# Scan output products in one row shape, and modulation columns one round later, in a two-layer hybrid block

## What is computed

```
for layer in 0, 1:
    mods = silu(c) @ w_mod[layer] + b_mod[layer]        # 6 * 1024 values, for latent and for context
    h    = rmsnorm(x) * (1 + sc1) + sh1
    u, qa, ka, va, qn, kn, vn, gates = split(h @ w_in[layer])
    y    = readout(scan_forward(u)) + readout(scan_backward(u)) + d_skip * u    # 32 groups of 16 channels, 64 states
    branches = glu(y), attention(qa, ka, va), neighbourhood_attention(qn, kn, vn)
    x    = x + g1 * (gated_merge(branches, gates) @ w_out)
    x    = x + g2 * mixture_of_experts(rmsnorm(x) * (1 + sc2) + sh2)            # 16 experts, top 2
```

## Time and profile before

| | us |
|---|---|
| median of 3 runs | 1943.32 (1941.05 to 1944.64) |
| the profiled execution | 1942.77 |
| its span, first to last instruction | 1941.1 |
| PE busy | 1762.7 |
| mean granted TensorE clock | 0.952 of full |
| layer 0: z of round 1 starts | 196.35 |
| layer 0: z of round 5 starts, attention starts | 274.48, 329.92 |
| layer 1: z of round 1 starts, attention starts | 1286.13, 1401.45 |

### The profile page before, as it was taken

One profiled execution on the slowest core, in us unless ns is written; L12 is line 12 of the kernel. 1 busy time (PEld: TensorE's weight loads), 2 busy tenths in 40 slices (PEclk: granted clock), 3 DMA queues, 4 the chain that ended last, 5 costly groups with the idle time before them and its releaser, 6 DMA issues.

```text
span 1941.1 us, 25808 instructions
## 1 busy us (share of the span) xinstructions
PE 1762.7 (91%) x9800; PEld 1064.2 (55%) x9800; DVE 656.6 (34%) x1410; ACT 411.4 (21%) x846; POOL 337.1 (17%) x314
## 2 busy tenths in 40 slices
PE   5999998889999999999979798999789999997796
PEld 2567555554444444555546446766458886554463
DVE  4669442660110113211101367775281113110012
ACT  3111111552000003222212231111152002221122
POOL 0004352870000001100000110425291000000000
PEclk9999897999999999999999898999699999999898
DMA  9313258309221243699999421144543367999992
GB/s 387 109 44 114 76 189 296 85 23 349 106 108 65 94 188 130 250 389 345 387 395 388 140 86 66 44 168 139 196 63 126 135 250 280 346 383 394 386 380 89
DMA packets 113523, 397.32 MB, mean 205 GB/s; under 512 B 42992, under 2 KB 62448, under 8 KB 74256
## 3 DMA queue, kind: packets, MB, share of 16 engines
q1 hardware_dynamic: 55920, 327.04, 43.8%
q10 hardware_dynamic: 50720, 29.54, 6.2%
q0 software_dynamic: 6784, 39.33, 6.0%
HBM read 369.65 MB, written 38.80 MB: 210 GB/s over the span
## 4 chain that ended last, share of the span: by engine, by line
PE 61%; DMA 11%; DVE 10%; SPq 6%; POOL 5%; issue 4%; ACT 2%; ACTq 1%; POOLq 0%; DVEq 0%
PE tile_ps L547 54%; SPq L492 6%; DMA arena<-sorted_in 4%; PE turn_ps L547 4%; DMA ring<-in_wpack 3%; POOL arena L1724 2%; DMA vn<-in_wpack 2%; PE out_ps L547 1%; ACTq L1086 1%; DMA arena<-arena 1%; PE turn_ps L772 1%; DVE arena L1592 1%; DVE x L1659 1%; DMA x<-in_xT 1%; DVE rstd L1365 1%
## 5 line engine op out<-in xcount | busy, mean ns | idle before, releaser
L547 PE MATMUL tile_ps<-h,ring 128*128 128x512 f32 (+1 forms) x1312 | 471.9, 514 | 3.9 <-ACT h L965 1.9
L547 PEld LDWEIGHTS tile_ps<-h,ring 128*128 128x128 f32 x1312 | 249.1, 192 | 214.1 <-issue 198.8
L547 PE MATMUL tile_ps<-arena 64*16 64x128 f32 (+4 forms) x1984 | 257.4, 376 | 31.2 <-ACT arena L1180 11.4
L547 PE MATMUL tile_ps<-arena,ring 128*128 128x512 f32 (+1 forms) x704 | 235.4, 486 | 2.7 <-issue 2.7
L547 PEld LDWEIGHTS tile_ps<-arena 128*64 128x64 f32 (+3 forms) x1984 | 165.1, 162 | 95.1 <-issue 64.9
L547 PEld LDWEIGHTS tile_ps<-arena,ring 128*128 128x128 f32 x704 | 133.9, 190 | 96.3 <-issue 87.4
L1724 POOL TENSOR_SCALAR arena<-arena,smx 128x512 f32<-128x512 f32 (+1 forms) x96 | 129.0, 1360 | 81.4 <-DVE smx L1578 81.1
L547 PE MATMUL tile_ps<-ring,arena 128*64 128x256 f32 (+1 forms) x624 | 97.4, 454 | 11.3 <-ACT arena L1180 7.1
L1156 ACT ACTIVATE arena<-tile_ps 128x512 f32<-128x512 f32 (+1 forms) x56 | 27.4, 490 | 347.4 <-PE tile_ps L547 347.4
L1650 DVE TENSOR_TENSOR arena<-tile_ps,arena 64x256 f32<-64x256 f32 x40 | 16.6, 416 | 225.0 <-ACT arena L1177 225.0
L1613 DVE TENSOR_TENSOR arena<-tile_ps,arena 128x512 f32<-128x512 f32 (+1 forms) x32 | 17.9, 558 | 212.1 <-PE tile_ps L547 212.1
(11 more groups left out here) (272 smaller groups left out, 2259.1 us busy)
## 6 DMA issues: line engine op xcount, KB each, us to landing
ring<-in_wpack SPq DMA_DIRECT2D x176, 1024.0 KB, 8.5
arena<-in_wpack SPq DMA_DIRECT2D x64, 1024.0 KB, 17.4
h<-in_wpack SPq DMA_DIRECT2D x15, 1024.0 KB, 26.0
qa<-in_wpack SPq DMA_DIRECT2D x12, 1024.0 KB, 14.7
qn<-in_wpack SPq DMA_DIRECT2D x12, 1024.0 KB, 17.1
kn<-in_wpack SPq DMA_DIRECT2D x12, 1024.0 KB, 20.0
vn<-in_wpack SPq DMA_DIRECT2D x12, 1024.0 KB, 22.1
sorted_out<-arena ACTq DMA_DIRECT2D x80, 128.0 KB, 7.5
```

Of the source, the lines that this page charges most:

```text
L547: return nc.tensor.matmul(out, lhsT, rhs, start=start, stop=stop)
```

## The change

- The `tm` product of each group is cut in two over its rows: the lower 64 go into bank y, the upper 64 into bank yb. All products of y and yb are then over 64 rows, in pairs of a lower and an upper one. Their number rises from 40 to 48 instructions for a round.
- mc of this layer's block is moved from its own round to the next one, behind y and yb (in round 8, ahead of them). DVE's use of it moves too.
- mr of this layer's block is moved behind the projections of its round; ACT copies its rows behind the projections.
- The next layer's blocks in layer 0 (rounds 5 to 7) come ahead of this layer's mr, and block 3 comes in round 8 (mr ahead of the last y, mc behind it) and no longer in the attention.
- The list of banks and the order of the slots follow. A round of nine is z, z, y, yb, mc, qk_ms, projection, mr, rope.

```diff
-IN_ROUND = {5: 0, 6: 1, 7: 2}
-IN_STEP = {1: 3}
+IN_ROUND = {5: 0, 6: 1, 7: 2, 8: 3}
+
+def next_mod(l, q):
+    return [IN_ROUND[q]] if l + 1 < LAYERS and q in IN_ROUND else []
...
     (order of the slots)
-    for q in range(NQ):
-        steps += mod(l, MOD1 + q)
+    for q in range(NQ + 1):
+        for n in next_mod(l, q):
+            steps += mod(l + 1, n)
         for job in in_loop(fill, q):
             steps += projected(job)
+        if q < NQ:
+            steps += mod(l, MOD1 + q)
...
     (TensorE)
+                def late_modulation(q):
+                    modulation_columns(l, MOD1 + q - 1)
+                    for n in next_mod(l, q):
+                        modulation(l + 1, n, l)
...
+                    if q == NQ:
+                        late_modulation(q)
...
-                            mm(bank(fwd)[:, cols], tm[:, o % 2, g, :], ug[:, G, :], True, False)
+                            for d, to in ((lower, fwd), (upper, bwd)):
+                                mm(bank(to)[:, cols], tm[d, o % 2, g, :], ug[d, G, :], True, False)
...
-                                b = mm(bank(bwd)[:, cols], co[upper], s, r == 0, r == 1)
+                                b = mm(bank(bwd)[:, cols], co[upper], s, False, r == 1)
                         full(fwd, f)
                         full(bwd, b)
+                    if 0 < q < NQ:
+                        late_modulation(q)
...
-                    if q < NQ:
-                        modulation(l, MOD1 + q, l)
+                    for n in next_mod(l, q):
+                        modulation_columns(l + 1, n)
                     for job in in_loop(fill, q):
                         projection(job, c0)
                     if q < NQ:
-                        modulation_columns(l, MOD1 + q)
+                        modulation(l, MOD1 + q, l)
...
-                    if l + 1 < LAYERS and q in IN_ROUND:
-                        modulation(l + 1, IN_ROUND[q], l)
-                        modulation_columns(l + 1, IN_ROUND[q])
...
     (ScalarE)
+                    if q == NQ:
+                        for n in next_mod(l, q):
+                            copy_rows(l + 1, n)
                     if q:
                         job = (l, "y", q - 1)
                         copy(job, ...)
+                    if q < NQ:
+                        for n in next_mod(l, q):
+                            copy_rows(l + 1, n)
...
+                    for job in in_loop(fill, q):
+                        copy_projection(job, c0)
                     if q < NQ:
                         copy_rows(l, MOD1 + q)
-                    for job in in_loop(fill, q):
-                        copy_projection(job, c0)
```

More of the change, by code:

```diff
@@ L210, in tile_jobs @@
             names += [(l, "z", q, 0), (l, "z", q, 1)] if q < NQ else []
-            names += [(l, "y", q - 1), (l, "yb", q - 1)] if q else []
+            late = [(l, "mc", MOD1 + q - 1)] if q else []
+            late += [(l + 1, "mr", n) for n in next_mod(l, q)]
+            out = [(l, "y", q - 1), (l, "yb", q - 1)] if q else []
+            names += out + late if q < NQ else late + out
             names += [(l, "qk_ms", q)] if q <= KW else []
+            names += [(l + 1, "mc", n) for n in next_mod(l, q)]
+            names += in_loop(fill, q)
             names += [(l, "mr", MOD1 + q)] if q < NQ else []
-            names += in_loop(fill, q)
-            names += [(l, "mc", MOD1 + q)] if q < NQ else []
             names += [(l, "rope", q)] if q <= KW else []
-            names += mod_jobs(l + 1, [IN_ROUND[q]]) if l + 1 < LAYERS and q in IN_ROUND else []
         n_pairs = len(attention_pairs(l))
@@ L220, in tile_jobs @@
             names += [(l, "sc", u, 0), (l, "sc", u, 1)] if u < n_pairs else []
-            names += mod_jobs(l + 1, [IN_STEP[u]]) if l + 1 < LAYERS and u in IN_STEP else []
         for kind, *at in mix_order():
@@ L761, in _ @@
                                                         qq[a:a + HD, q0:q0 + P], kk[a:a + HD, 0:nk]))
-                    early = l + 1 < LAYERS and n in IN_STEP
-                    if early:
-                        modulation(l + 1, IN_STEP[n], l)
                     if LAG <= n < len(us) + LAG:
@@ L774, in _ @@
                             ins.then_inc(turn_full[half], 1)
-                    if early:
-                        modulation_columns(l + 1, IN_STEP[n])
                     if n > LAG:
@@ L1093, in _ @@
                             head_squares(l, q + 1, c0)
+                    for job in in_loop(fill, q):
+                        copy_projection(job, c0)
                     if q < NQ:
                         copy_rows(l, MOD1 + q)
-                    for job in in_loop(fill, q):
-                        copy_projection(job, c0)
-                    if l + 1 < LAYERS and q in IN_ROUND:
-                        copy_rows(l + 1, IN_ROUND[q])
                 for q in range(NQ):
@@ L1130, in _ @@
                                       y_dram[:, t].rearrange("j p c -> p j c")).then_inc(y_in, 16)
-                    if l + 1 < LAYERS and n in IN_STEP:
-                        copy_rows(l + 1, IN_STEP[n])
                     B = n - LAG - 2
@@ L1529, in _ @@
                         carry_in(q)
+                    if q == NQ:
+                        modulation_block(l, MOD1 + q - 1)
                     if q:
@@ L1536, in _ @@
                         free(job, TT(v, v, bank(job)[:, 0:GQ * NCH], ALU.add))
+                    if 0 < q < NQ:
+                        modulation_block(l, MOD1 + q - 1)
+                    for n in next_mod(l, q):
+                        modulation_block(l + 1, n)
                     t = c0 if q < KW else 0
@@ L1544, in _ @@
                         STT(v[:, t:], v[:, t:], g, qrs[:, t:], ALU.mult, ALU.mult).then_inc(qnorm_done, 1)
-                    if q < NQ:
-                        modulation_block(l, MOD1 + q)
                     if q <= KW:
@@ L1555, in _ @@
                         TT(v[:, CTX:], v[:, CTX:], qrt[:], ALU.add).then_inc(rope_done, 1)
-                    if l + 1 < LAYERS and q in IN_ROUND:
-                        modulation_block(l + 1, IN_ROUND[q])
                 us = pairs[l]
@@ L1583, in _ @@
                             .then_inc(turn_free[0], 1)
-                    if l + 1 < LAYERS and n in IN_STEP:
-                        modulation_block(l + 1, IN_STEP[n])
                     part = n - len(us) // 2 + 2
```

## The result

The changed kernel takes 1963.6 us (median of 4 runs, 1958.8 to 1964.1) beside 1943.2 us for the kernel before (4 runs timed beside it, 1941.05 to 1944.64): a ratio of 1.010, 95% interval 1.0082 to 1.0119. It is slower by 20 us, where I had forecast 11 less. Its profiled execution took 1963.89 us, with a span of 1962.2, 21.1 more than before.

What follows compares the result with a forecast made beforehand. PE was taken to bound the kernel, with ACT's copy of y and POOL's circle limiting loop rounds. Terms +3.5 + 1 - 4.2 - 5.5 - 6.2 = -11.4 us gave 1931.4 (1932 in the median's terms), range 1920 to 1944.

Steps and rivals of the forecast that it cites:

- The y products: Scan loops: a group of y falls from 0.99 to 0.66 us, 1.3 us less a round, 21 us if all on the path.
- Where the first rounds stand still: Rounds 1 to 4: projection waits for ACT's copy of y behind eight DMAs; layer 0 77.0 us at full clock, before 78.1.
- rival B: Loops: every y saving is on the path, the copy of y not holding the projection: 1914 us, chance 0.12.
- the half clock's price in rounds 1 to 4: After the new idle before projections: 4.5 us in layer 0 (0 to 10), 0.7 for each of three rounds in layer 1.
- my 14.85: Layer 1, rounds 1 to 4: a round takes 14.85 us by ACT's copy, against 13.7 by POOL's circle alone.
- rival D: Rounds 1 to 4: new idle before each projection puts all following products at half clock; slower, 1950 us, chance 0.10.
- the landing of tm in rounds 5 to 8: Layer 0: tm lands slowly behind earlier weight loads, 11.83 us as before; the rounds still take 50 against 55.4, -5.5 us.
- the 47.6: Layer 0: attention starts 47.6 us behind z of round 5, slow tm landing and the moved block included, half clock not.
- The moved block: Layer 1's block 3 leaves layer 0's attention, -6.2 us (-3.5 to -6.5); its new place is counted in the late rounds.
- Round 0: Layer 0 gains nothing, as rope already waits for DVE; in layer 1 the 0.8 us is real.

Runs made afterwards that it cites:

- e1: The kernel before with only the tm products cut in two pairs of 64 rows: 1936.4 us, ratio 0.995.
- e4: The changed kernel with ACT's copy of y ahead of its eight DMA issues in rounds 1 to 4: 1937.1 us, ratio 0.995 to the kernel before.
- f5: The changed kernel with three dummy products ahead of the projection in rounds 1 to 4: 1946.2 us, ratio 0.9995 to the kernel before.
- e2: The changed kernel with the tm products whole again, order and moved block kept: 1959.1 us, ratio 1.007 to the kernel before.
- f7: The changed kernel with weight loads held until round 5's transfer of tm has landed: 1955.4 us, ratio 1.006 to the kernel before.
- g2: The changed kernel with ACT's copy of y first and the weight loads held until round 5's tm landed: 1933.4 us, ratio 0.994 to the kernel before.
- f6: The changed kernel with mr back ahead of the projection, mc still late: 1947.6 us, ratio 1.002 to the kernel before.
- e3: The kernel before with only the next layer's block 3 moved from attention to behind round 8's last y: 1944.3 us, ratio 0.999.
- f9: The kernel before with 64-row pairs and, in rounds 1 to 4, ACT's copy of y ahead of its eight issues: 1940.7 us, ratio 0.998.

## Why the prediction was wrong

**The y products: right.** z and y fell from 5.89 to 4.78 us; the 48 half loads of a y span 2.76 us in PEld's timeline, 0.69 a group beside the 0.66 worked out. Alone that is worth 10 us (e1), half of the 21 it would be with all of it on the path. In e1's rounds 1 to 4 of layer 0 the hole of 1.4 to 1.9 us takes it back.

**Where the first rounds stand still: right.** The projection waited 2.5 to 3.3 us in layer 0 and 2.0 to 4.3 us in layer 1 for the copy of y, not for its operands; rival B is out. It isn't the copy itself that holds the bank (0.37 us) but the eight issues ahead of it (5.1 to 6.7 us): e4, which only swaps them, has no hole. Even the sums without half clock held: 77.0 us were worked out for layer 0's four rounds, and f5, at 1.00 in most of them, took 77.2; in layer 1 61.0 stand beside 62.8. In part that is luck: round 1 was worked out as 20.5 from ACT's times in a round at half clock and took 19.1, round 3 as 19.0 and took 20.3.

**The failed step: the half clock's price in rounds 1 to 4.** I took half of the old price in layer 0 (4.5 us) and 0.7 us for each of three rounds in layer 1. The four projections of layer 0 took 9.7, 8.8, 8.8 and 8.5 us, 7.4 over 28.4; those of layer 1 took 6.6, 6.2, 5.7 and 5.4, 9.1 over 14.8. Layer 1 round 2 is the clearest: 8.8 + 6.2 + 2.4 = 17.4, my 14.85 with nothing wrong but the projection. f5 gives the whole as 17.5 us, where I had 4.5 + 2.1. It was rival D's mechanism, which I gave 0.10, though only the projection ran in part at half clock and not all that follows; the rounds grew by 2.0 and 2.5 us each, under the 3 from which I had said it decides, and it decided all the same, since the other gains weren't there. My argument against it, that round 4 ran at 1.00 with idle time inside, read the row wrongly: that idle time was 0.3 us, behind 1.93 us of dense mr. The Trainium skill's rule that I had set beside rival D (TensorE: Matmul & The Clock Gate, A second HAM failure mode: short idles between groups of products make the clock swing) is what happened behind the hole; f5, which changes nothing but what PE does in the hole, agrees with it by a granted clock of 1.00 in round 2 of layer 1, against 0.80 in the changed kernel. But I had called round 1 of the kernel before, at 0.77, a case of it, and that was wrong: PE was busy for all 21.73 us of that round. The half clock there, and in e2, came without idle time, and what brings it on then stays open.

**The second: the landing of tm in rounds 5 to 8.** I took 11.8 us for it and had it hidden in the 47.6. It took 13.4, y waited 5.5 us for it, and the half clock followed: +1.9 instead of -5.5 in layer 0. Behind z of round 5, y started at 21.5 where I had 16, z of round 7 at 35.9 for 28, the last y at 53.5 for 44, attention at 57.4 for 47.6 (50 with my half clock). In layer 1 I had a late transfer for the last y only; round 5's took 11.4 us, and the stretch -0.3 instead of -4.2. The cause, that the slots are released earlier, in round 4, I had named for layer 0 only. f7 shows it by its landing, g2 and f6 by their rounds.

**The moved block.** -6.2 was forecast, and -6.8 came between the scores. Its new place was counted inside the 47.6, and in the changed kernel it is small: mr and mc stand around the last y with no wait between them, 2.8 us together. What I had at nothing is that attention's next steps give about 3 us back in this trace. So the block was worth about 1 us, and e3, with the block in a slightly worse place, shows no gain clear of the noise.

**Round 0**: right in both layers (nothing, and 0.9).

By terms: 4.5 us in layer 0's first rounds, 8.1 in layer 1's (with round 0), 7.4 and 3.9 in the late rounds, about 2.4 in the block, together 26 us on -11.4, gives +15. The other 6 lie outside the loops, and above all behind the last: from layer 1's first scores to the end the kernel before took 539.7 us, the changed one 546.0. The twelve experiments, in which that part's code is the same, took 541.6 to 547.0 there, with 543.2, 544.3 and 546.0 in e1, e3 and f9, which have the old order, and I count this as scatter between executions; no run shows where it comes from. All twelve lie above the 539.7 of the one traced execution of the kernel before. So the 21 us between the two profiled executions hold some microseconds that no part of the change explains.

## What to carry to other kernels

When products are taken out of the stretch ahead of a wait, ask what PE does between its last dense block and the end of that wait. With the dense mr ahead of a hole of 1.4 to 1.9 us the next block kept the clock in seven rounds of eight (e1); with thin products ahead of a hole of 2.0 to 4.3 us it lost it in all eight. A hole of 2.5 to 2.9 us cost another 1.7 to 2.5 us in the products behind it, and a mend as small as a copied bank ahead of eight issues, or dummy products, gave it back. A block moved from one place of the chain to another gains only what the new place hides, and a slot released earlier starts its load earlier, ahead of small transfers that someone waits for.

## What the runs showed of the hardware

The half clock came without any idle time of PE in e2: behind z and y of 5.89 us, mc took 1.86 for 1.05 and qk_ms 2.06 for 1.10; and in the kernel before, rounds 1 to 3 of layer 0. In e4 the same thin products behind z and y of 4.8 us ran at full clock.

The last transfer of tm took 13.36 and 11.44 us behind weight loads of 1 MB each, on another engine's queue; with these loads held it took 2.02 (f7).

Two of VectorE's additions were slower beside GpSimd's. Timeline of DVE, changed kernel, layer 1, round 1:

```profile
1296.42 1.40 DVE L1361 TENSOR_TENSOR arena<-arena 128x224 f32<-128x224 f32 x1
1297.86 1.40 DVE L1362 TENSOR_TENSOR arena<-arena 128x224 f32<-128x224 f32 x1
```

and of POOL:

```profile
1296.09 1.49 POOL L1715 TENSOR_TENSOR arena<-arena 128x640 f32<-128x640 f32 x1 [31.63 <-PE tile_ps L550]
1297.66 1.36 POOL L1716 TENSOR_TENSOR arena<-arena 128x640 f32<-128x640 f32 x1
```

In the kernel before, where POOL began only when they were done, these additions took 0.39 us. Here each began beside a GpSimd operation (which ends at 1297.58 and 1299.02) and ended 0.24 us behind its end, at 1297.82 and 1299.26. The Trainium skill (SBUF — State Buffer, Who interferes with whom) has a VectorE instruction with two inputs in SBUF contend with a GpSimd instruction that reads SBUF, over a shared pair of ports with an exclusive lock; these rows agree, by the additions' 1.40 us for 0.39. POOL began 5.0 us behind z here and 6.3 before, since y ended earlier, and so met additions that it used to pass.
